# A keys-and-values stage: other order of its slabs, of its input's normalisation and of the next stage's first transposes

## The reference

```
def _shared_kv(h, kv_norm, kv_w, cmp_pos, cmp_w1, cmp_b1, cmp_w2, k_norm):
    kv = (_rmsnorm(h, kv_norm) @ kv_w).reshape(b, s, 6, 4, 64)      # six slots, four groups of 64
    k_cmp = _rmsnorm(_compress(kv[0], cmp_pos[0], cmp_w1[0], cmp_b1[0], cmp_w2[0]), k_norm[0])
    v_cmp = _compress(kv[1], cmp_pos[1], cmp_w1[1], cmp_b1[1], cmp_w2[1])
    k_sel, v_sel = _rmsnorm(kv[2], k_norm[1]), kv[3]                # blocks left out
    k_win, v_win = _rmsnorm(kv[4], k_norm[2]), kv[5]
# _compress: blocks of 32 tokens, one every 16 (15 of them), flattened: gelu(flat @ w1 + b1) @ w2
# then: h = h + 0.5 * _swiglu(_rmsnorm(h, ffn_norm[1, 0]), w_gate_up, w_down)
```

## Time and profile before

| | us |
|---|---|
| median of 3 runs | 1710.79 |
| lowest, highest | 1709.71, 1717.64 |
| the profiled execution | 1709.71 |
| its span, first to last instruction | 1708.0 |
| PE busy in the span | 1659.3 (97%) |
| DVE, ACT, POOL busy | 966.1, 746.6, 32.5 |
| mean granted clock of TensorE | 0.98 of full speed |

### The profile page before, as it was taken

One profiled execution on the slowest core, in us unless ns is written; L12 is line 12 of the kernel. 1 busy time (PEld: TensorE's weight loads), 2 busy tenths in 40 slices (PEclk: granted clock), 3 DMA queues, 4 the chain that ended last, 5 costly groups with the idle time before them and its releaser, 6 DMA issues.

```text
span 1708.0 us, 19549 instructions
## 1 busy us (share of the span) xinstructions
PE 1659.3 (97%) x8230; PEld 1389.6 (81%) x8230; DVE 966.1 (57%) x1016; ACT 746.6 (44%) x910; POOL 32.5 (2%) x53
## 2 busy tenths in 40 slices
PE   7999999998999998999999999999999989999998
PEld 6888898867788887888898888888888877888887
DVE  5555556876755546555557555467555444556552
ACT  5444244655344424444334434346444333544441
POOL 0000000000000000000000000000000020000000
PEclk9999999999999999999999999999999986999999
DMA  8564474423565645564565555566564440046551
GB/s 265 180 222 178 155 259 136 136 93 129 161 197 181 226 152 179 187 207 177 171 210 173 184 185 202 183 200 207 174 208 179 166 165 1 1 126 220 180 189 74
DMA packets 226088, 291.11 MB, mean 170 GB/s; under 512 B 10517, under 2 KB 203729, under 8 KB 225873
## 3 DMA queue, kind: packets, MB, share of 16 engines
q1 hardware_dynamic: 226000, 289.87, 51.0%
HBM read 288.78 MB, written 1.05 MB: 170 GB/s over the span
## 4 chain that ended last, share of the span: by engine, by line
PE 83%; DVE 9%; ACT 3%; issue 2%; DMA 2%; POOL 1%; SPq 0%; DVEq 0%; POOLq 0%; ACTq 0%
PE bank L1537 24%; PE bank L1539 24%; PE bank L1538 24%; DVE w_lo L984 3%; PE bank L1993 2%; PE bank L1698 2%; PE bank L1546 1%; ACT w_hi L632 1%; PE bank L2018 1%; POOL stats L576 1%; DVE z_sb L1046 1%; DVE x_sb L1017 1%; PE bank L2003 1%; DMA raw<-in_w_in_dram 1%; DVE bn L1024 0%
## 5 line engine op out<-in xcount | busy, mean ns | idle before, releaser
L984 DVE TENSOR_TENSOR w_lo<-raw,w_hi 128x2048 fp32r<-128x2048 f32 (+1 forms) x268 | 607.8, 2274 | 334.5 <-ACT w_hi L632 333.3
L632 ACT ACTIVATE w_hi<-raw 128x2048 fp32r<-128x2048 f32 (+1 forms) x268 | 507.9, 1901 | 192.0 <-DMA raw<-in_ffn_w_down_dram 97.8
L1537 PE MATMUL bank<-w_hi,xT_lo 128*128 128x512 f32 (+1 forms) x1360 | 539.5, 397 | 8.9 <-DVE w_lo L984 6.1
L1539 PE MATMUL bank<-w_hi,xT_hi 128*128 128x512 f32 (+1 forms) x1360 | 531.0, 390 | 0.0
L1538 PE MATMUL bank<-w_lo,xT_hi 128*128 128x512 f32 (+1 forms) x1360 | 530.1, 390 | 0.0
L1537 PEld LDWEIGHTS bank<-w_hi,xT_lo 128*128 128x128 f32 x1360 | 257.7, 189 | 61.4 <-issue 8.8
L1539 PEld LDWEIGHTS bank<-w_hi,xT_hi 128*128 128x128 f32 x1360 | 257.2, 189 | 53.9
L1538 PEld LDWEIGHTS bank<-w_lo,xT_hi 128*128 128x128 f32 x1360 | 257.9, 190 | 50.2
L1537 PE MATMUL bank<-w_hi,hT_lo 128*128 128x512 f32 x528 | 206.5, 391 | 0.0
L1539 PE MATMUL bank<-w_hi,hT_hi 128*128 128x512 f32 x528 | 205.6, 389 | 0.0
L1538 PE MATMUL bank<-w_lo,hT_hi 128*128 128x512 f32 x528 | 205.5, 389 | 0.0
(11 more groups left out here) (249 smaller groups left out, 1244.5 us busy)
## 6 DMA issues: line engine op xcount, KB each, us to landing
raw<-in_ffn_w_gate_up_dram SPq DMA_DIRECT2D x176, 512.0 KB, 4.8
raw<-in_ffn_w_down_dram SPq DMA_DIRECT2D x132, 512.0 KB, 4.0
raw<-in_ffn_w_gate_dram SPq DMA_DIRECT2D x44, 512.0 KB, 4.0
raw<-in_ffn_w_up_dram SPq DMA_DIRECT2D x44, 512.0 KB, 5.0
raw<-in_w_in_dram SPq DMA_DIRECT2D x44, 512.0 KB, 4.9
raw<-in_conv_w_in_dram SPq DMA_DIRECT2D x24, 512.0 KB, 4.5
raw<-in_kv_w_dram SPq DMA_DIRECT2D x12, 512.0 KB, 4.2
raw<-in_w_out_dram SPq DMA_DIRECT2D x8, 512.0 KB, 3.7
```

The lines of the kernel that those rows point to most:

```text
L632: nc.scalar.activation(w_hi[:, slot, 0:width], raw[:, slot, 0:width], ACT.Copy).then_inc(high_ready, 1)
L984: nc.vector.tensor_tensor(w_lo[:, slot, 0:width], raw[:, slot, 0:width], w_hi[:, slot, 0:width].bitcast(F32), ALU.subtract).then_inc(low_r ...
L1537: nc.tensor.matmul(o, x_lo, wh, start=first, stop=False, skip_group_check=shared)
L1539: return nc.tensor.matmul(o, x_hi, wh, start=False, stop=last_one, skip_group_check=shared)
```

## The change

Nothing is computed otherwise. What moves:

- Slab order: the pair of slots 0 and 1 is now loaded as slabs 4 and 5 and used after four blocks of the other pairs for token tile 0 and two for tile 1. The second token tile's blocks of slabs 2 and 3 come after the features. Buffers 2 and then 3, 4 and 5 together are given back there, and a semaphore of its own (`cmp_in_psum`) tells ACT that the features are done.
- The squares and RMS norm for the next FFN move from behind slab 5's split to behind slab 9's, and the second key slot's squares and scaling in front of the splits of slabs 8 and 9.
- `next_input` for the next FFN: tile 0 behind the whole compression, tile 1 inside the FFN, which now starts by token tile (`by_token` with `first_tiles`); `transpose_hidden(1)` and `compressed()` stand between its half slabs.
- ACT and DVE copy out that input at `kv == 1` and after it, with slab 11's and 12's splits ahead.

```diff
--- before.py
+++ after.py
@@ SP
-                    for d, (pair, kh) in enumerate(((1, 0), (1, 1), (2, 0), (0, 0), (0, 1), (2, 1))):
-                        load(s0 + d, columns(w, kh, [(512 * pair, 256), (512 * pair + 256, 256)]))
-                    gains(n)
+                    def two_slots(slab, pair):
+                        for kh in range(2):
+                            load(s0 + slab + kh, columns(w, kh, [(512 * pair, 256), (512 * pair + 256, 256)]))
+                    two_slots(0, 1)
+                    two_slots(2, 2)
+                    two_slots(4, 0)
...
                         if kv == 0:
+                            gains(n)
@@ ACT
                     split_to(s0 + 5)
-                    for tt in range(NT):
-                        norm(n, [tt])
...
-                    keys_out(0, 2)
-                    split_to(s0 + 8)
-                    act.wait_ge(slab_used, s0 + 5)
+                    keys_out(0)
+                    split_to(s0 + 7)
+                    act.wait_ge(cmp_in_psum, 1)
...
+                    keys_out(1)
                     split_to(s0 + 9)
-                    keys_out(1, 6)
-                    evacuate_input(inputs_before(n + 1), TOKENS_FIRST[0:2])
-                    split_to(s0 + 10)
...
+                    for tt in range(NT):
+                        norm(n, [tt])
+                    for kv in range(2):
+                        split_to(s0 + 10 + 2 * kv)
                         act.wait_ge(slab_used, s0 + 8 + 2 * kv)
                         nc.scalar.activation(hid_row[:, kv, :], bank[6 + kv][0:CMP_ROWS, 0:CMP_HID], ACT.Copy).then_inc(hid_rows, 1)
+                        if kv == 1:
+                            evacuate_input(inputs_before(n + 1), TOKENS_FIRST[0:2])
                         act.wait_ge(bias_ready, kv + 1)
...
-                    hidden_out(0)
                     evacuate_input(inputs_before(n + 1), TOKENS_FIRST[2:4], 2)
-                    split_to(s0 + 11)
-                    hidden_gelu(0)
-                    hidden_out(1)
-                    split_to(s0 + 12)
-                    hidden_gelu(1)
                     split_to(s0 + 13)
@@ DVE
                     split_to(s0 + 5)
-                    for tt in range(NT):
-                        rms_norm(n, tt)
...
-                    split_to(s0 + 8)
+                    split_to(s0 + 7)
...
-                    split_to(s0 + 9)
                     keys_spread(1)
                     keys_norm(1)
-                    evacuate_input(inputs_before(n + 1), TOKENS_FIRST[0:2])
-                    split_to(s0 + 10)
-                    evacuate_input(inputs_before(n + 1), TOKENS_FIRST[2:4], 2)
+                    split_to(s0 + 9)
+                    for tt in range(NT):
+                        rms_norm(n, tt)
                     for kv in range(2):
-                        split_to(s0 + 11 + kv)
+                        split_to(s0 + 10 + 2 * kv)
+                        if kv == 1:
+                            evacuate_input(inputs_before(n + 1), TOKENS_FIRST[0:2])
                         dve.wait_ge(hidT_psum, kv + 1)
...
                     ins.then_inc(hid_v_ready, 1)
+                    evacuate_input(inputs_before(n + 1), TOKENS_FIRST[2:4], 2)
                     split_to(s0 + 13)
@@ PE, FFN behind KV
                         def work(tt):
+                            if behind_kv(n) and (j, kh, tt) == (1, 0, 0):
+                                pe.wait_ge(key_normed, 2)
                             gate_up(j, kh, [tt])
+                            if behind_kv(n) and (j, kh, tt) == (0, 0, 0):
+                                transpose_hidden(1)
+                            if behind_kv(n) and (j, kh, tt) == (0, 0, 1):
+                                compressed()
...
-                    elif behind_kv(n):
-                        pe.wait_ge(xT_ready, 4 * inputs_before(n) + 4)
-                        gate_up(0, 0)
-                        transpose_hidden(1)
-                        gate_up(0, 1)
-                        compressed()
-                        pe.wait_ge(key_normed, 2)
-                        tile(1)
@@ PE, KV
-                    by_token(n, [lambda tt, d=d: keys_values(d, d // 2, d % 2, tt) for d in range(3)], 2)
+                    by_token(n, [pairs(slot, kh) for slot in range(2) for kh in range(2)], 2)
                     for kh in range(2):
-                        feature_slab(s0 + 3 + kh, kh, [bank[4], bank[5]], 4).then_inc(slab_used, 1)
-                    for tt in range(NT):
-                        keys_values(5, 1, 1, tt)
-                    pe.wait_ge(key_normed, 1)
-                    next_input(n + 1, 0)
+                        ins = feature_slab(s0 + 4 + kh, kh, [bank[4], bank[5]], 4)
+                    ins.then_inc(cmp_in_psum, 1)
+                    keys_values(1, 0, 1).then_inc(slab_used, 1)
+                    keys_values(1, 1, 1).then_inc(slab_used, 3)
...
-                            if kv == 0 and part == 1:
-                                pe.wait_ge(xc_ready, 9)
-                                next_input(n + 1, 1)
                             if kv == 1 and part == 0:
                                 transpose_hidden(0)
+                    pe.wait_ge(key_normed, 1)
+                    next_input(n + 1, 0)
```

More of the change, by code:

```diff
@@ L200, in two_block_kernel @@
         loaded_kv = sem("loaded_kv")
+        cmp_in_psum = sem("cmp_in_psum")
         xc_high = sem("xc_high")
@@ L611, in key_roots_behind @@
                     key_roots(0)
+                if kind == KV:
                     key_roots(1)
@@ L619, in _ @@
                 if kind == KV:
-                    key_roots_behind()
                     pool.wait_ge(kc_spread, 1)
@@ L1915, in _, with keys_values, pairs, work @@
                 if kind == KV:
-                    def keys_values(d, slot, kh, tt):
-                        ins = token_slab(s0 + d, kh, 512, slice(0, 512), lambda tt: bank[2 * slot + tt][:], tiles=[tt])
-                        if tt == NT - 1:
-                            ins.then_inc(slab_used, 1)
-                    by_token(n, [lambda tt, d=d: keys_values(d, d // 2, d % 2, tt) for d in range(3)], 2)
-                    for kh in range(2):
-                        feature_slab(s0 + 3 + kh, kh, [bank[4], bank[5]], 4).then_inc(slab_used, 1)
-                    for tt in range(NT):
-                        keys_values(5, 1, 1, tt)
-                    pe.wait_ge(key_normed, 1)
-                    next_input(n + 1, 0)
+                    def keys_values(slot, kh, tt):
+                        return token_slab(s0 + 2 * slot + kh, kh, 512, slice(0, 512), lambda tt: bank[2 * slot + tt][:], tiles=[tt])
+                    def pairs(slot, kh):
+                        def work(tt):
+                            if tt == 0:
+                                keys_values(slot, kh, 0)
+                            elif slot == 0:
+                                keys_values(slot, kh, 1).then_inc(slab_used, 1)
+                        return work
+                    by_token(n, [pairs(slot, kh) for slot in range(2) for kh in range(2)], 2)
+                    for kh in range(2):
+                        ins = feature_slab(s0 + 4 + kh, kh, [bank[4], bank[5]], 4)
+                    ins.then_inc(cmp_in_psum, 1)
+                    keys_values(1, 0, 1).then_inc(slab_used, 1)
+                    keys_values(1, 1, 1).then_inc(slab_used, 3)
                     for kv in range(2):
```

8 lines of the change are left out of this document (3 added, 5 removed).

## The result

The changed kernel takes 1728.06 us in the median of four runs (1725.92 to 1729.75), the kernel before beside it 1711.24 (1709.71 to 1717.64): ratio 1.0091, 95% interval 1.0074 to 1.0108: slower, by about 0.9%. Forecast were 1727.0 and 1719 to 1733. The profiled execution took 1726.31 us, its span is 1724.6, 16.6 longer than before.

The account below looks back on a forecast made before the run. TensorE (PE), busy 97% and never waiting in this stretch, was taken as the bound, so the change could only open waits: 1.4 + 8.4 + 2.4 + 2.6 + 2.6 = 17.4 us on 1709.7 gave 1727.1, stated as 1727; range 1719 to 1733.

Parts of the forecast that it names:

- A: Compression: PE waits 1.4 us for slab 8's low half, which stands on DVE behind xc_lo and second key scaling.
- B: First matmul of the next FFN: PE waits 8.4 us for its transposed input, queued late on ACT and DVE.
- D: Clock fall with the long wait for the FFN's input: slow matmuls after it lose 2.6 us.
- C: In the next FFN: PE waits 2.4 us for slab 13's low half, behind the second token tile's input copies.
- E: Second clock fall, at the wait for slab 13: 2.6 us lost, at better than even odds.
- The start, slabs 0 to 5: nothing.: Start of the keys-and-values stage: the new slab order costs PE no time.
- The sign to look for on ACT: ACT's idle time in front of the first GELU grows from 2.96 us to about 6.
- the 0.7 of the alternative: Clock fall early in the long wait, mostly over when PE returns: 0.7 us lost, sum 1.9 us lower.
- One fall or none: Rivals on the clock: one fall, 1724.5 us, chance 0.30; no lasting fall, 1721.9 us, chance 0.09.
- The loads bind: Rival: four slabs requested within 5 us land late, adding 2 to 3 us, about 1730 us; chance 0.10.
- Not slower: Rival: FFN input passes at once, its wait only the bare passage, 1.2 us; 1714.7 us or no change; chance 0.08.
- the point that the rival named: ACT must reach its input copies by 1177.2, 5.6 us earlier than worked out, for the input to pass at once.

Follow-up runs that it names:

- e1: Kernel before with only the new order and return of slabs, old input hand-over kept: 1715.32 us, ratio 1.0003, stage 80.8 us.
- e3: Changed kernel with the second key slot's scaling moved behind slab 9's split: 1730.98 us, ratio 1.0091, stage 94.7 us.
- e4: Changed kernel with the next input's squares and RMS norm back behind slab 5's split: 1724.63 us, ratio 1.0060, stage 88.3 us.
- e5: Changed kernel with the first token tile's input copies ahead of the splits of slabs 11 and 12: 1726.58 us, ratio 1.0063, stage 85.4 us.
- e8: Changed kernel with slab 13's split ahead of the second token tile's input copies: 1724.34 us, ratio 1.0046, stage 87.7 us.
- e6: Changed kernel with 28 unused matmuls in the long wait for the FFN's input: 1730.34 us, ratio 1.0093, stage 89.0 us.
- e9: Changed kernel with the edits of e4, e5 and e8 together: 1716.08 us, ratio 0.9993, stage 80.6 us.
- e7: Kernel before with unused matmuls in three waits of other stages (start, 658, attention): 1700.43 us, ratio 0.9919, stage 75.4 us.

## Why the prediction was right, step by step

| term | forecast | measured |
|---|---|---|
| A, slab 8's low half | 1.4 | 1.48 |
| clock behind A | 0 | 1.1 (4.59 - 3.5) |
| B, the FFN's input | 8.4 | 6.96 |
| D, clock behind B | 2.6 | 2.2 (4.94 - 2.73) |
| C, slab 13's low half | 2.4 | 2.23 |
| E, clock behind C | 2.6 | 1.7 (3.4 us at the half) |
| sum | 17.4 | 15.7, of 16.5 in the stage |

- **The start, slabs 0 to 5: nothing.** It held for PE: from slab 0 to the compression there is no wait. But e1 shows that the slab order costs 5.4 us on its own under the old hand-over, through the late high halves of slabs 8 and 9. In the changed kernel the key scaling stands where DVE would have waited for them: the two low halves take 4.71 us in a row, against 4.49 for slabs 11 and 12, so 0.2 us are left of it in DVE's queue. "Nothing" held because of term A.
- **A** stood where it was forecast and as long, and e3, which moves the key scaling, removes it. Slab 9 was 1.4 us late, which I had not: ACT began its high half at 1167.22, which is 1167.5 in the clock of before, for 1166.1 forecast, behind a wait that ends with a DMA.
- **B's** chain was right almost to the tenth. The subtraction was to start at 1184.9 and started at 1184.62, in a trace in which the stage runs 0.3 earlier. Two of its parts were measured, each taken out alone: the norms, 3.1 of it (e4), and the two splits, 5.5 (e5). They don't add up, since with one gone something else in the chain sets the time. B itself was 1.4 us shorter because PE reached it 1.2 us late, by the clock's fall behind A that I hadn't foreseen. That is the mis-sized step, a term put at nothing, and it is neutral: what A's fall cost, B's wait gave back. The sign to look for on ACT was mis-worked too: its idle time ahead of the first GELU is 3.28 us and not about 6. By the forecast's own times, hidden row done at 1172.9 and bias at 1178.0, it would have been 5.1, and in it stands a table load of 1.28 us (1173.30) that the forecast left out; before, it stood ahead of the GELU too.
- **C and E.** Both there. e8 takes both away, 3.9 us. Its stage lost 4.2, but this is no closer check: A's fall, 1.1, is missing there too, B is 0.4 longer, and 0.5 for the hidden row is new.
- **D.** The clock was low when PE came back after 7 us, as the row at 14.03 had said, and twelve matmuls lost 2.2 us, not the 0.7 of the alternative. e6, in which PE had work in the wait, had no fall. The trace agrees with the Trainium skill, "TensorE: Matmul & The Clock Gate", Part 1 (What's actually happening), by which activity is what releases the low clock. What the prediction left open, a fall that is over before PE comes back, is settled by e3: the clock was at half from 1186.0, 6.3 us of the wait and 3.6 us of matmuls, so it did not rise while PE was idle.
- **What is left,** 0.8 us of 16.5, I couldn't assign from the idle times alone. Counted from start to start, slab 8's matmuls with A's wait cost 2.76 us more than 3.47, the transposes with B and the first twelve matmuls 9.42 more than 3.52, and slab 13's with C 4.08 more than 5.47: 16.3 in sum. So 0.6 of the 0.8 are PE's restarts at the three waits, and 0.2 is left.
- **Rivals.** One fall or none: refuted in this execution, there were three. The loads bind: PE waited for no DMA, though ACT did, 1.17 and 2.25 us, which DVE's queue hid; e1 and e3 show that this lateness costs as soon as the key scaling does not stand ahead of the splits. Not slower: e5 and e9 show that with the copies ahead of the splits B is indeed close to the bare passage, 1.48 and 0.98 for 1.2, which is the point that the rival named; the stage was still 10.0 and 5.2 us longer than before's.

The sum was 1.7 us too high for its own terms and the 0.8 that no idle time shows made up half of that: B, D and E were 1.4, 0.4 and 0.9 too large (C 0.2), the clock behind A 1.1 too small. So 1727.0 for 1728.06 owes something to errors of both signs; that the stage is longer, by how much to some 2 us, and where, does not. The whole time owes more to luck: the sum stands on one execution of before of 1709.7 us, and 35 of 57 later ones took 1715.4 or more. Had the changed kernel had as large a share of longer executions, its median would lie several us higher, near the upper end of the range or beyond it. It did not (23 of its 28 took under 1730), for a reason that no run shows.

## What to carry to other kernels

With in-order engines, moving a step later on the engine that bounds the kernel puts its result behind whatever stands next in the *other* engines' text: walk their queues in order, and price the wait as the sum of what is ahead. Copy out what the bounding engine waits for before doing the weights it needs later. When that engine must wait, matmuls of no use can keep the clock up (e6's long wait, 658 in e7), and then the wait costs the wait alone. Read a change of this size by the stage in the traces: the kernel before had executions of two kinds, some 9 us apart, and a ratio of medians compares how often each came up.

## What the runs showed of the hardware that I had not expected

- A wait of 1.48 us in the compression was followed by a fall (after, e4 and e5), though one of 1.89 had none in the earlier trace rows. In e6, e8 and e9 the same wait had none, nor had the 2.2 us one in e6. So the length of the one wait doesn't decide it; what does was not settled. The fall can also come when the wait is over: about 1 us after PE's return in e4's longest wait, 3.84 us, and at after's third.
- At the program's start the granted clock reads 1.00, but the twelve matmuls from 14.03 to 19.28 run at half pace, 0.43 us each (window of before):

```profile
14.00:19.30 5.30, 5.27 (x13) 4.14 (x14) 3.98 (x2) 3.10 (x3) 0.00 (x0) 1.00 1.10 348
```

  With 18 fillers ahead of them (e7) the pace is 0.23 us for each from the second on. There the pace, and not the clock's row, is the witness.
- Fillers that read 128 columns of bf16 four times over (e7) kept the clock at 1.00 in the wait at 658, as those in the full format did in e6. In the attention, where it was low already, it rose while they ran.
